# Sums over partitions for the modulation columns as four one-column matmuls, and three chunks placed by block in two runs

## What is computed

```
c_act = jax.nn.silu(c)
for i in range(DEPTH):
    mod = c_act @ ada_w[i] + ada_b[i]
    sh1, sc1, g1, sh2, sc2, g2 = [m[:, None, :] for m in jnp.split(mod, 6, axis=-1)]
    h = x * (1.0 + sc1) + sh1
    y = s5_mixer(h, ...) if i % N_MIXERS == 0 else dsa_mixer(h, ...)
    x = layer_norm(ALPHA * x + (1.0 + g1) * y, ln_g[i, 0], ln_b[i, 0])
    h = x * (1.0 + sc2) + sh2
    x = layer_norm(ALPHA * x + (1.0 + g2) * swiglu(h, ffn_w_in[i], ffn_w_out[i]), ln_g[i, 1], ln_b[i, 1])
```

## Time and profile before

| what | value |
|---|---|
| median of three runs | 2504.74 us |
| the profiled execution, device time | 2504.74 us |
| its span | 2503.0 us |
| TensorE busy | 96% of the span |
| VectorE busy | 75% |
| ScalarE busy | 42% |
| memory traffic, mean | 251 GB/s |

### The profile page before, as it was taken

The page is one execution under the profiler, slowest core; times in us unless marked ns, Lnnn a source line. Parts: engine busy times, 40 slices in busy tenths (PEclk is TensorE's granted clock), DMA queues, the critical chain, the costliest instruction groups (busy, mean ns, idle before and its releaser), DMA issues.

```text
span 2503.0 us, 33077 instructions
## 1 busy us (share of the span) xinstructions
PE 2393.0 (96%) x12489; PEld 1926.8 (77%) x12489; DVE 1875.3 (75%) x2992; ACT 1039.9 (42%) x1230; POOL 35.3 (1%) x67
## 2 busy tenths in 40 slices
PE   5898879999999999999999999989999999999998
PEld 1575468878888888888878888768888888888886
DVE  6576988977778888889878987887787755455457
ACT  1354034364443444344464434464644344443442
POOL 0000000000000000000000000000000000000000
PEclk9999889999999999999999999999999999999999
DMA  9896838867888998899758886636698766556664
GB/s 339 327 321 230 341 97 296 304 200 264 300 292 281 334 328 278 288 323 322 256 172 268 286 276 218 225 101 205 214 310 292 232 193 190 187 189 195 192 220 142
DMA packets 314685, 627.35 MB, mean 251 GB/s; under 512 B 30656, under 2 KB 31072, under 8 KB 314272
## 3 DMA queue, kind: packets, MB, share of 16 engines
q1 hardware_dynamic: 310240, 611.35, 71.3%
q0 software_dynamic: 4288, 13.90, 2.0%
HBM read 623.05 MB, written 2.10 MB: 250 GB/s over the span
## 4 chain that ended last, share of the span: by engine, by line
PE 87%; DVE 7%; DMA 2%; ACT 1%; SPq 1%; issue 1%; DVEq 0%; ACTq 0%
PE psA L2016 41%; PE psB L2016 40%; DVE prod L1385 2%; PE psT L1674 1%; DVE tmp L1390 1%; DVE st L1396 1%; DMA col_raw<-in_ada_w 1%; PE psM L1706 1%; DMA w_raw<-in_s_in_w 1%; DVE w_lo L1048 0%; SPq L602 0%; DMA w_raw<-in_ffn_w_in 0%; PE psT L1874 0%; ACT stgA L825 0%; SPq L578 0%
## 5 line engine op out<-in xcount | busy, mean ns | idle before, releaser
L1048 DVE TENSOR_TENSOR w_lo<-w_raw,w_hi 128x1024 fp32r<-128x1024 f32 x740 | 902.6, 1223 | 496.7 <-ACT w_hi L749 492.1
L749 ACT ACTIVATE w_hi<-w_raw 128x1024 fp32r<-128x1024 f32 x740 | 783.3, 1060 | 1111.5 <-PE psB L2016 489.3
L2016 PE MATMUL psB<-w_hi,hT_hi 128*128 128x512 f32 x1040 | 406.7, 391 | 0.0
L2016 PE MATMUL psA<-w_hi,hT_hi 128*128 128x512 f32 x1008 | 398.3, 395 | 8.4 <-issue 3.2
L2016 PE MATMUL psB<-w_hi,hT_lo 128*128 128x512 f32 x1040 | 404.8, 389 | 0.0
L2016 PE MATMUL psB<-w_lo,hT_hi 128*128 128x512 f32 x1040 | 404.7, 389 | 0.0
L2016 PE MATMUL psA<-w_hi,hT_lo 128*128 128x512 f32 x1008 | 393.8, 391 | 0.0
L2016 PE MATMUL psA<-w_lo,hT_hi 128*128 128x512 f32 x1008 | 393.4, 390 | 0.0
L1065 DVE SCALAR_TENSOR_TENSOR ada_acc<-ada_raw,csil,ada_acc 128x512 f32<-128x512 f32 x450 | 336.1, 747 | 12.4
L2016 PEld LDWEIGHTS psA<-w_hi,hT_hi 128*128 128x128 f32 x1008 | 189.8, 188 | 51.7 <-issue 8.8
L2016 PEld LDWEIGHTS psB<-w_hi,hT_hi 128*128 128x128 f32 x1040 | 195.3, 188 | 43.3 <-issue 2.0
(11 more groups left out here) (370 smaller groups left out, 2295.3 us busy)
## 6 DMA issues: line engine op xcount, KB each, us to landing
w_raw<-in_ffn_w_in SPq DMA_DIRECT2D x352, 512.0 KB, 4.6
ada_raw<-in_ada_w SPq DMA_DIRECT2D x480, 256.0 KB, 5.3
w_raw<-in_ffn_w_out SPq DMA_DIRECT2D x176, 512.0 KB, 4.7
col_raw<-in_ada_w SPq DMA_DIRECT2D x128, 512.0 KB, 6.6
w_raw<-in_dsa_in_w SPq DMA_DIRECT2D x112, 512.0 KB, 4.6
w_raw<-in_s_glu_w SPq DMA_DIRECT2D x64, 512.0 KB, 5.4
w_raw<-in_s_in_w SPq DMA_DIRECT2D x32, 512.0 KB, 5.5
w_raw<-in_dsa_out_w SPq DMA_DIRECT2D x32, 512.0 KB, 4.9
```

Source lines behind the costliest of these rows:

```text
L749: nc.scalar.activation(high(u), w_raw[:, u % RING], ACT.Copy).then_inc(w_hi_ready, 1)
L1048: V.tensor_tensor(low(u), w_raw[:, u % RING], high(u).bitcast(F32), ALU.subtract).then_inc(w_lo_ready, 1)
L2016: ins = MM(PS[s][:, t, 0:r.width], a_[:, kt, tok], b_[:, kk, 0:r.width], start=kt == 0 and m == 0, stop=k == r.units - 1 and kk == UK - 1 ...
```

## The change

There are two edits. First, every column chunk is summed as chunks 0 and 1 were: the 18 column chunks 2, 3 and 12 to 27 lose the split, the two matmuls with ones, the multiplication with the identity and the reduction. They get the four one-column matmuls, and the short addition now reads PSUM. The 12 gate chunks keep the split and the two matmuls. Second, the three chunks of the `glu` run (2, 3, 4) and the three of the `rope` run (22, 23, 24) are placed by block (`ada`) instead of evenly (`dense`). At the start of `glu` the steps of positions 1 to 3 are issued together with the one of position 4, after the wait for `y_full`.

```
-        glu = Run("glu", 4, s5_glu_w[0], (D, 0), dense=(EARLY, 3, 13, 5), before="s5")
+        glu = Run("glu", 4, s5_glu_w[0], (D, 0), ada=[(0, 3, 2)], before="s5")
-                runs += [Run("rope", 4, dsa_in_w[0], (0, NB), layer=1, dense=(22, 3, 4, 19), before="ln"),
+                runs += [Run("rope", 4, dsa_in_w[0], (0, NB), layer=1, ada=[(1, 4, 22)], before="ln"),
+        def rows_to(q):
+
+            return sum(streamed(k)[3] is not None for k in range(q + 1))
...
-                                if r is glu and (q_, k) == (EARLY, 0):
-                                    sp.wait_ge(y_full, len(PIECES))
-                                if r.before == "ln" and (q_, k) == (r.dense[0], 0):
-                                    sp.wait_ge(w_used, product(r, 0, 0))
                                 ada_unit(q_, k)
                         if q is not None:
+                            first = r is glu and i == 0
+                            if first and n == RING:
+                                sp.wait_ge(y_full, len(PIECES))
                             if i == 1 and n == 0 and r.before == "ln":
                                 sp.wait_ge(w_used, product(r, 0, 0))
                             for k in range(AU):
-                                if k in ada_at(n, r.per):
+                                if k in ada_at(n, r.per) and not (first and n < RING):
+                                    ada_unit(q, k)
+                                elif first and n == RING and any(k in ada_at(m, r.per) for m in range(RING)):
                                     ada_unit(q, k)
...
-                if k == AU - 1 and q >= EARLY:
+                if k == AU - 1 and streamed(q)[3] is not None:
                     vec.wait_ge(ada_used, u + 1)
...
-                    if q >= EARLY:
-                        link(V.tensor_tensor(diagonal[:], M[:, 1].rearrange("p (j c) -> p j c", c=P),
-                                             ident[:].unsqueeze(1).to_broadcast([P, AW // P, P]), ALU.mult))
-                        link(V.reduce_sum(picked[:], diagonal[:], AXX))
-                    V.tensor_tensor(modcol[:, c:c + AW // P], modcol[:, c:c + AW // P],
-                                    picked[:] if q >= EARLY else M[:, 1, 0:AW // P], ALU.add
+                    V.tensor_tensor(modcol[:, c:c + AW // P], modcol[:, c:c + AW // P], M[:, 1, 0:AW // P], ALU.add
                                     ).then_inc(chunk_stored, 1)
...
-                if q >= EARLY:
-                    pe.wait_ge(acc_split, q - EARLY + 1)
+                if streamed(q)[3] is not None:
+                    pe.wait_ge(acc_split, rows_to(q))
                     MM(M[:, 1], ones[:], acc_hi[:], start=True, stop=False)
                     ins = MM(M[:, 1], ones[:], acc_lo[q % 2][:], start=False, stop=True)
```

More of the change, by code:

```diff
@@ L144, in build @@
         acc_hi = at("acc_hi", "brow", [P, AW], F32R, plus=2 * K)
-        diagonal = at("diagonal", "brow", [P, AW // P, P], plus=2 * K)
         acc_lo = [at(f"acc_lo{n}", "ada_acc", [P, AW], F32R, plus=n * 2 * K) for n in range(2)]
@@ L244, in build @@
         best = at("best", "small", [P, 8], plus=704)
-        picked = at("picked", "small", [P, AW // P], plus=736)
         logit = at("logit", "stgA", [P, 4, SEQ])
@@ L707, in _ @@
                                             pattern=[[P, TOK], [-1, SEQ]], channel_multiplier=1).then_inc(constants, 1)
-                if r.dense and r is not glu:
+                if r.dense:
                     for q in range(r.dense[0], r.dense[0] + r.dense[1]):
@@ L711, in _ @@
                     continue
-                if not r.ada and r is not glu:
+                if not r.ada and r.kind != "glu":
                     continue
@@ L721, in _ @@
                     if q is not None:
-                        load_brow(q)
-                if r is glu:
-                    for q in range(r.dense[0], r.dense[0] + r.dense[1]):
                         load_brow(q)
```

## The result

| kernel | median us | range, executions | ratio to before, 95% interval |
|---|---|---|---|
| before | 2505.56 | 2504.47 to 2508.5, 4 | |
| after | 2526.24 | 2523.53 to 2528.16, 4 | 1.0073 [1.0061, 1.0085] |

By these medians the change costs 20.7 us. The forecast was 2512.5 us, with a range of 2508.5 to 2516: the direction was right, the size was not, and some 11 to 13 us were not in the sum. The profiled execution took 2526.05 us, its span is 2524.3 us, 21.3 more than the span before.

The account below looks back on a forecast made before the run. The prediction took TensorE to bound the kernel where the chunks change. From 2504.74 us it added 8.2 for the sums, took off 0.4 for shorter waits and counted edit 2 as nothing: 2512.5 us, range 2508.5 to 2516.

Parts of the forecast that it names:

- Edit 1, TensorE's side: At the 18 column-chunk sums: each costs TensorE 0.46 us more, 8.2 us in all, bounds 6.3 to 10.8.
- a gap that goes by columns alone: Rival at the 18 sums: one-column matmuls cost next to nothing, 8.2 us of old sums gained, 2496.1 us; chance 0.03.
- Edit 1, VectorE's side: VectorE loses 2.5 us per column chunk, 45 us in all, worth nothing in the stretches where TensorE does not wait.
- the 0.4 us of gain: Shorter TensorE waits at the end of `glu` and the start of attention, together 0.4 us, bounds 0 to 3.2.
- Edit 2: Placement by block in `glu` and `rope`: VectorE and the DMA engines keep up at 1.45 steps a position; cost nothing.
- The likeness to `ff`: The same placement already runs from 571 to 704 us without a TensorE pause; `rope` was taken to be like it.
- The start within edit 2: Start of `glu`: weight unit 5 waits behind six chunk transfers, with about 3 us to spare; cost nothing.
- The rival of the burst: Start of `glu`: six chunk transfers ahead of unit 5 pause TensorE 1 to 4 us, 2513.5 to 2516.5 us; chance 0.07.
- What would show it: Signs in the new trace: sums at 1.36 us, VectorE down about 45 us; a pause near 377 us shows the burst.

Follow-up runs that it names:

- e8: e1 with each of a sum's four matmuls streaming 128 equal columns of ones instead of one; 2511.32 us, ratio 1.0027.
- e1: The kernel before with only the new sums, chunks of `glu` and `rope` left evenly spread; 2513.71 us, ratio 1.0036.
- e2: The changed kernel with the old sums, so only the placement by block in `glu` and `rope`; 2518.58 us, ratio 1.0050.
- e9: e2 (old sums) with the chunk transfers of `glu` and `rope` issued two positions later; 2507.64 us, ratio 1.0008.
- e7: The changed kernel with SyncE issuing the chunk transfers of `glu` and `rope` two positions later; 2512.28 us, ratio 1.0030.
- e5: e1 with 1.45 chunk steps a position in `glu`, still `dense`, so issued two positions later; 2514.05 us, ratio 1.0036.
- e16: The changed kernel, 8 ring places, chunk transfers issued two positions later in the first block of `glu` alone; 2519.16 us, ratio 1.0052.
- e3: The kernel before with only the chunks of `glu` placed by block, `rope` left dense, old sums; 2515.01 us, ratio 1.0039.
- e13: The changed kernel with a ring of 12 places instead of 8 for the late chunks, same order of issue; 2518.29 us, ratio 1.0054.
- e14: e13 with the saved-up chunk transfers at the start of `glu` put behind weight unit 7; 2518.29 us, ratio 1.0055.

## Why the prediction was right or wrong

**Edit 1, TensorE's side: right.** 0.46 us a sum forecast, 0.45 measured by the same count and 0.49 by the longer one, 8.2 to 8.8 us for 18, inside the bounds of 6.3 to 10.8. The choice to count to the third main matmul was right; the count to the second would have said 0.35. For these matmuls, each with new weights, a gap that goes by columns alone is refuted twice, by the rows and by e8.

**Edit 1, VectorE's side: right where chunks are evenly spread.** 39 us less of VectorE (45 forecast) bought nothing that shows in e1, and of the 0.4 us of gain there is no trace larger than the spread. Where `glu` is placed by block the relief is worth some 3 us: `glu` loses 10.5 us in e2 and 7.6 with the new sums, and 2.8 in e9 and none in e7. The forecast treated the two edits apart and had no such term.

**Edit 2: wrong, and this is the step that failed.** The forecast put it at nothing: "together 2.3 of 2.72 us, so it keeps up", "New is only the start", "So I cost the start at nothing". It cost 11 to 14 us. The rates were no error (e5 runs them for nothing). Left out was the place in SyncE's list: an `ada` step stands behind the unit of its own position, a `dense` one two positions later. It stood in the description of the kernel before and in no term of the sum. Two positions are the whole of the price (e7, with the new sums). The likeness to `ff`, which runs by block without a pause, was taken as proof. But SyncE blocks in `ff` too. Its waits for ring places in the kernel before, from 600 to 700 us:

```profile
SPq L568 <- DVE ada_acc L1065: 22.3, 16, 2.5
SPq L568 <- DVE ada_acc L1062: 17.4, 3, 6.2
```

That is 39.7 us for ring places, up to 6.2 at a time, behind which TensorE never pauses. That the weight units had just enough slack there is what TensorE's full windows say; how much, no run measures. The likeness holds for a state that is already filled, not for a start that has to catch up. e16 says the same of `glu` itself.

**The start within edit 2: the right place, too small.** The rival of the burst (0.07) named the right mechanism and put 1 to 4 us on it. Its count, unit 5 issued at 365.6, landed at 371.2 and needed at 377.0, took the issues at 0.44 us; they took 0.58 each for the six and 1.86 for the unit. The unit landed 5.5 us later than counted, of which 1.1 are the later start of `glu` and some 3.4 its landing in 9.0 instead of 5.6 us, and its `w_lo` was ready at 379.05 instead of 373.5. More important, the count stopped at unit 5. Unit 8 was issued only at 380.11, behind the stand of 6.9 us. The same count for the start of `rope` was not made, nor one for a lower clock behind a pause, 1.8 to 1.9 us twice. An estimate made afterwards: SyncE standing for as long as VectorE has for two positions, 5.4 us, at each place where the weight units start without a lead, here `glu` and `rope`, bounds the term by 0 to 11 us; the traces show 11.7 over e1. That they meet is in part luck, since the 11.7 hold 3.7 us of clock, and the pause in `rope` has no such stand in its chain.

**What would show it.** The text named a pause near 377 us as the sign of the burst. It is there, 379.10 with 0.69 us. The larger one, which ends at 399.04, and that in `rope` it did not name.

## What to carry to other kernels

When a step moves in the list of a queue that issues in order, count for its new place how many transfers are wanted in flight (positions between issue and use, times steps per position) and set that against the ring: if it is more, the queue stands there, and everything behind it goes late, needed or not. Whether that costs time depends on the lead of what stands behind: 40 us of such waits were free in `ff`, and the price here was paid where the weight units had just started. A full engine elsewhere with the same placement proves only that its slack was enough there, so look at the queue's own waits in that place. A matmul of few columns with weights of its own is priced as one with a weight load, 0.1 us here, not by its columns.

## What the runs showed of the hardware

A pause of TensorE of 2.9 us was followed by a window of 11 us with a mean granted clock of 0.84 and cost 1.9 us on top of itself. So were pauses of 2.7 us (e3, ending at 396.43) and 2.0 us (after, 1361.22); pauses of 2.3 us (e13, 381.66), 2.0 us (e14, 397.59) and 0.7 us (after, 379.10) were followed by 1.00. The issue of a transfer on SyncE, 0.44 us in the earlier trace rows, took 0.58 us in the row of six and 1.86 us for the one right behind them. Weight units took 8.1, 10.2 and 10.4 us to land where the DMA engines were full (363 to 390 GB/s), against 5.6 in the median before. Engines as full as that did not by themselves stop TensorE (e7, 394 and 386 GB/s with TensorE busy throughout).
